# Windowed attention of a diffusion step: the loop over five query tiles written out as ten half tiles, with the next half's scores and exponentials issued ahead

## What is computed

```python
def _attend(q, k, v, valid, sink):
    s = jnp.einsum('bqgrd,bkgd->bgrqk', q, k).astype(jnp.float32) * (HEAD_DIM ** -0.5)
    if valid is not None:
        s = jnp.where(valid[None, None, None], s, NEG_INF)
    ...
    p = jax.nn.softmax(jnp.concatenate([s, sk], axis=-1), axis=-1)[..., :-1]
    return jnp.einsum('bgrqk,bkgd->bqgrd', p.astype(v.dtype), v)
```

## Time and profile before

| | |
|---|---|
| median of 3 runs | 5891.16 us (5883.75 to 5902.05) |
| the profiled execution's own time | 5885.15 us |
| its span | 5883.4 us |
| PE, PEld, DVE, ACT, POOL busy | 92%, 89%, 56%, 37%, 36% |
| attention of layer 0, first mask transfer to the end of the last copy | 385.32 to 504.83 us |
| attention of layer 1, the same | 3259.32 to 3379.23 us |

### The profile page before, as it was taken

How to read it: one execution, slowest core, us unless ns; L and a number is a source line. 1 busy time by engine, 2 the same in 40 slices (tenths; PEclk the granted TensorE clock), 3 DMA queues, 4 the chain that set the end, 5 groups by cost and what they waited for, 6 DMA issues and landing times. The chain is left out here.

```text
span 5883.4 us, 118582 instructions
## 1 busy us (share of the span) xinstructions
PE 5435.2 (92%) x47828; PEld 5219.4 (89%) x47828; DVE 3268.5 (56%) x6068; ACT 2201.4 (37%) x2769; POOL 2128.6 (36%) x968
## 2 busy tenths in 40 slices
PE   5977889899999999999989688889999999999999
PEld 2856779899999999999978477889999999999998
DVE  4545648665655156665645465586555631665665
ACT  4434322455555522222233433225555563222221
POOL 0001122466656443433400022136556654333332
PEclk8988999999999999999999799999999999999999
DMA  5200022355555564454411001124555546445443
GB/s 205 87 32 13 4 94 75 120 174 179 172 179 176 187 205 168 164 173 169 143 73 53 18 8 61 62 90 153 179 175 178 177 164 228 168 166 175 165 165 109
DMA packets 303987, 777.56 MB, mean 132 GB/s; under 512 B 23724, under 2 KB 109228, under 8 KB 299496
## 3 DMA queue, kind: packets, MB, share of 16 engines
q1 hardware_dynamic: 303592, 771.94, 38.7%
HBM read 586.52 MB, written 185.34 MB: 131 GB/s over the span
## 5 line engine op out<-in xcount | busy, mean ns | idle before, releaser
L2138 POOL TENSOR_TENSOR ex_v_lo<-ex_v_raw,ex_v_hi 128x1024 fp32r<-128x1024 f32 x256 | 691.6, 2723 | 1072.8 <-ACT ex_v_hi L2044 1072.8
L355 PE MATMUL ex_ps<-tk_h_hi,tk_u_hi 128*128 128x320 f32 x4096 | 965.7, 317 | 46.6 <-POOL tk_u_lo L2126 34.9
L2126 POOL TENSOR_TENSOR tk_u_lo<-tk_u_raw,tk_u_hi 128x1024 fp32r<-128x1024 f32 x256 | 642.2, 2509 | 883.3 <-ACT tk_u_hi L2014 862.0
L355 PE MATMUL ex_ps<-ex_wa_hi,ex_v_hi 128*128 128x320 f32 x4096 | 935.7, 310 | 18.8 <-issue 18.8
L355 PE MATMUL ex_ps<-tk_h_hi,tk_u_lo 128*128 128x320 f32 x4096 | 937.1, 310 | 0.0
L355 PE MATMUL ex_ps<-tk_h_lo,tk_u_hi 128*128 128x320 f32 x4096 | 935.8, 310 | 0.0
L355 PE MATMUL ex_ps<-ex_wa_lo,ex_v_hi 128*128 128x320 f32 x4096 | 935.1, 310 | 0.0
L355 PE MATMUL ex_ps<-ex_wa_hi,ex_v_lo 128*128 128x320 f32 x4096 | 934.9, 309 | 0.0
L2298 DVE TENSOR_TENSOR ex_y<-ex_y,ex_ps 128x640 f32<-128x640 f32 x496 | 405.9, 818 | 672.5 <-PE ex_ps L355 667.1
L355 PEld LDWEIGHTS ex_ps<-tk_h_hi,tk_u_hi 128*128 128x128 f32 x4096 | 679.0, 189 | 50.2 <-POOL tk_u_lo L2126 35.8
L355 PEld LDWEIGHTS ex_ps<-ex_wa_hi,ex_v_hi 128*128 128x128 f32 x4096 | 686.8, 188 | 19.3 <-issue 19.3
(11 more groups left out here) (326 smaller groups left out, 7836.7 us busy)
## 6 DMA issues: line engine op xcount, KB each, us to landing
tk_u_raw<-in_expert_u SPq DMA_DIRECT2D x256, 512.0 KB, 4.3
ex_v_raw<-in_expert_v SPq DMA_DIRECT2D x256, 512.0 KB, 3.3
act_spill<-tk_act_e SPq DMA_DIRECT2D x256, 320.0 KB, 2.3
grid_scratch<-tk_grid SPq DMA_DIRECT2D x160, 512.0 KB, 5.6
ex_g<-grid_scratch SPq DMA_DIRECT2D x64, 1280.0 KB, 10.6
x<-in_w_mod_rows SPq DMA_DIRECT2D x192, 256.0 KB, 5.1
ex_a<-act_spill SPq DMA_DIRECT2D x32, 1280.0 KB, 6.9
x<-act_spill SPq DMA_DIRECT2D x32, 1280.0 KB, 6.9
```

What stands on the lines that cost most here:

```text
L355: ins = nc.tensor.matmul(out[:, q, 0:HALF], a, b[:, q * HALF:(q + 1) * HALF], start=(first and n == 0), stop=(last and n == 2))
L2126: nc.gpsimd.tensor_tensor(u_lo[:, at % 2], u_raw[:, at % 3], u_hi[:, at % 2].bitcast(F32), ALU.subtract).then_inc(e["u_split"], 1)
L2138: nc.gpsimd.tensor_tensor(v_lo[h][:, k], v_raw[:, k], v_hi[h][:, k].bitcast(F32), ALU.subtract).then_inc(e["v_split"], 1)
```

## The change

The loop over tiles with its five stages becomes one stage without a loop. Its unit is the half tile: `part` 0 to 9, four heads each. The copies to `qs`, `ks`, `vs` are gone: with a constant index the matmuls read `z`, `k_tiles` and `v_tiles` directly. All five masks, 1280 KB, come in one transfer into the space of `rot`, which the stage before has finished with. `sm`, the buffer of scores and probabilities, has three slots of four heads, `ps_o` has two of one tile. Each engine's program does the next half's front work before the present half's back work. Nothing of the arithmetic is changed.

```diff
-        with nc.Fori(0, TILES) as m:
-            with stage(nc, "at_mask", "at_staged", "at_scores", "at_masked", "at_top", "at_exp",
...
+            @block.sync
+            def _(sp):
+                sp.dma_start(mask, s.d["masks"].rearrange("m p n -> p m n")).then_inc(mask_in, 16)
...
+                def score(part):
+                    m = part // 2
+                    for p in (2 * (part % 2), 2 * (part % 2) + 1):
+                        g = 8 * m + 2 * p
+                        if g >= 4:
+                            pe.wait_ge(masked, g - 2)
...
+                def turn(part, p):
+                    for n in (2 * p, 2 * p + 1):
+                        g = 4 * part + n % 4
+                        pe.wait_ge(probs, g + 1)
+                        if g >= 2:
+                            pe.wait_ge(pt_taken, g - 1)
...
+                def values(pair):
+                    m, p = pair // 4, pair % 4
+                    pe.wait_ge(pt_taken, 2 * pair + 2)
+                    if m >= 2:
+                        pe.wait_ge(out_taken, m - 1)
...
+                score(0)
+                for part in range(N):
+                    if part + 1 < N:
+                        score(part + 1)
+                    for q in range(2):
+                        turn(part, 2 * (part % 2) + q)
+                        if part or q:
+                            values(2 * part + q - 1)
+                values(2 * N - 1)
...
+                def front(part):
...
+                        dve.wait_ge(scores, 4 * part + h + 1)
+                        v.tensor_tensor_reduce(sm[:, part % SLOTS, h, :], ps_s[:, h, :], mask[:, part // 2, :], 1.0,
+                                               sink[:, h:h + 1], ALU.add, ALU.max, top[:, part, h:h + 1]).then_inc(masked, 1)
...
+                def back(part):
+                    dve.wait_ge(exped, 5 * part + 5)
...
+                def take(m):
+                    dve.wait_ge(out_ready, 8 * m + 8)
+                    v.tensor_copy(s.z[:, 0:4, m * P:(m + 1) * P], ps_o[:, m % 2]).then_inc(out_taken, 1)
...
+                front(0)
+                for part in range(N):
+                    if part + 1 < N:
+                        front(part + 1)
+                    back(part)
+                    if part and part % 2 == 0:
+                        take(part // 2 - 1)
+                take(TILES - 1)
...
+                exponents(0)
+                for part in range(N):
+                    if part + 1 < N:
+                        exponents(part + 1)
+                    copies(part)
```

More of the change, by code:

```diff
@@ L820, in attention @@
-        with nc.Fori(0, TILES) as m:
-            with stage(nc, "at_mask", "at_staged", "at_scores", "at_masked", "at_top", "at_exp",
[L822 to L834, removed]
+        ps_o = mem.enter_context(nc.psum_tensor("at_ps_o", [P, 2, 4, P], F32))
@@ L835, in values @@
                     for k in range(4):
                         for n in (2 * p, 2 * p + 1):
-                            v_k = (vs[:, k, :] if k < 3 else cv[:])[:, half(n)]
-                            ins = nc.tensor.matmul(ps_o[half(n), p, :], v_k, pt[:, n % 4, k * P:(k + 1) * P],
+                            v_k = (v_tiles[:, m + k, :] if k < 3 else cv[:])[:, half(n)]
+                            ins = nc.tensor.matmul(ps_o[half(n), m % 2, p, :], v_k, pt[:, n % 4, k * P:(k + 1) * P],
                                                    start=(k == 0), stop=(k == 3))
@@ L841, in values @@
                                 ins.then_inc(out_ready, 1)
[L843 to L881, removed]
-                        dve.wait_ge(masked, hs.stop)
-                        link(nc.vector.tensor_scalar(top[:, hs], top[:, hs], -1.0, None, ALU.mult))
-                        nc.vector.tensor_tensor(sink_e[:, hs], s.pvs("sink")[:, hs], top[:, hs],
-                                                ALU.add).then_inc(top_ready, 1)
-                    for n, hs in enumerate(head_halves):
-                        dve.wait_ge(exped, (n + 1) * (HEADS // 2 + 1))
-                        link(nc.vector.tensor_tensor(den[:, hs], den[:, hs], sink_e[:, hs], ALU.add))
-                        link(nc.vector.reciprocal(den[:, hs], den[:, hs]))
-                        for h in range(hs.start, hs.stop):
-                            nc.vector.tensor_scalar(sm[:, h, :], sm[:, h, :], den[:, h:h + 1], None,
-                                                    ALU.mult).then_inc(probs, 1)
-                    dve.wait_ge(out_ready, HEADS)
-                    nc.vector.tensor_copy(s.z[:, 0:4, bass.ds(m * P, P)], ps_o[:])
@@ new lines, in _, with exponents, copies @@
+            @block.scalar
+            def _(act):
+                def exponents(part):
+                    act.wait_ge(top_ready, part + 1)
+                    nc.scalar.activation(sink_e[:, part], sink_e[:, part], ACT.Exp).then_inc(exped, 1)
+                    for h in range(PART):
+                        nc.scalar.activation(sm[:, part % SLOTS, h, :], sm[:, part % SLOTS, h, :], ACT.Exp,
+                                             bias=top[:, part, h:h + 1], accum_out=den[:, part, h:h + 1]).then_inc(exped, 1)
+                def copies(part):
+                    for h in range(PART):
+                        g = 4 * part + h
+                        act.wait_ge(pt_ready, g + 1)
+                        if g >= 4:
+                            act.wait_ge(out_ready, g - 3)
+                        nc.scalar.activation(pt[:, h, :], ps_t[:, h % 2, :], ACT.Copy).then_inc(pt_taken, 1)
+                exponents(0)
[3 more added lines that the diff above has]
+                    copies(part)
```

67 lines of the change are left out of this document (44 added, 23 removed).

## The result

The changed kernel takes 5916.91 us, median of 7 runs (5908.67 to 5921.11), against 5891.79 for the kernel before on the same chip (7 runs). The ratio is 1.0032 with an interval of 1.0023 to 1.0041: **slower by 0.3%**, where I had said no change at 5882.5. (The two medians alone stand at 1.0043, a little above the interval of the recorded ratio; what follows needs only the direction.) The profiled execution took 5921.11 us with a span of 5919.3; before's span was 5883.4. The two profiles are 35.9 apart, the medians 25, since before's profiled execution was one of its short ones and the changed kernel's its longest.

What follows compares the result with a forecast made beforehand. No engine was full in attention; a chain passing between PE, DVE and ACT bounded it. Per layer 19.3 + 8 x 11.3 + 5.7 = 115.4 us, 8.6 less over both; forecast 5882.5 us, range 5858 to 5902.

Steps and rivals of the forecast that it cites:

- nothing else in the program moves: Whole kernel: barriers divide a layer's stages, so a microsecond saved in attention is one saved in the kernel.
- the long straight program loads late: Rival, attention: four additional rounds of code each cost a PE wait, at longest 6 us a layer; slower, chance 0.03.
- The half: Attention, one half tile: 10.1 us at full clock, 10.9 to 12.4 partly cold, mean 11.3, eight times a layer.
- two in nine: PE's clock in attention: after two of nine long pauses it stayed at 1.00; such halves cost 10.1 us.
- The order bound: Attention: DVE's `back` stands behind the next `front`, ACT's copies behind the next exponentials; turns wait some 3 us for DVE.
- the walk: Attention: step-by-step timing of one half through PE, DVE and ACT, from its first score; 10.1 us at full clock.
- The start: Attention's beginning: masks land at 5.2 us, first turn at 13.7, first half's values end at 19.3.
- the bounds: Attention's mask transfer: 1280 KB lands between 2.5 us, as 256 KB does, and 8.5, as 2560 KB does.
- The estimate of 7.7 us: Attention's mask transfer: 1280 KB by the skill's figure, making each layer 2.5 us longer; not used in the forecast.
- The clock did not hold: Rival, attention: PE's clock stays at 1.00 across pauses; halves 10.1 us, 104.9 a layer, 5861.6 in all; chance 0.35.
- The clock did not stay down: Rival, attention: PE cold throughout, 14.1 us a half, 142 a layer, 5936 us in all; chance 0.06.
- PE shows waits without a cause at regular distances: Sign in the changed trace that would show the prediction wrong; no size given.

Runs made afterwards that it cites:

- the loop put in place: Changed kernel with 96 more PE and 126 more DVE instructions, so the expert loops start elsewhere in a block: 0.9975, 5880.52 us.
- dummies: Changed kernel, expert loops moved by added code, with 16 unused identity turns in each of PE's nine attention pauses: 0.9953.
- the split transfer: Changed kernel, expert loops moved by added code, with the first tile's mask transferred by itself and the other four behind it: 0.9957.
- both together: Changed kernel, expert loops moved by added code; ACT copies before the next half's exponentials, DVE divides before masking the next half: 0.9920.
- ScalarE's by itself: Changed kernel, expert loops moved by added code; only ACT's order turned back, copies before the next half's exponentials: 0.9984.
- VectorE's by itself: Changed kernel, expert loops moved by added code; only DVE's order turned back, dividing before masking the next half: 1.0016.
- both additions: Kernel before with 40 PE instructions and 127 DVE memsets added ahead of the rotation of queries and keys: 1.0040.

## Why the prediction was wrong

**The step that failed** is a half sentence of the first part: "nothing else in the program moves". It was true of the diff and of the barriers between stages, and not of the place of the code. The stage's 1065 additional PE instructions moved the start of a later loop of 2940, whose first jump comes some 770 us behind attention. That cost 31.3 us over six jumps in the profiled executions, eleven times what attention gave. I had the jumps before me: before's list has 30.5 us for `issue` in the experts' matmuls, in 14 waits (two of them, 9.4 us each, outside the loop), and I looked only at those in the scan. The rival "the long straight program loads late" named the right resource at the wrong place, inside the stage, with at most 6 us a layer and a chance of 0.03. The sentence that I took from the Trainium skill (Runtime: NRT & Kernel Launch, Instruction fetch mechanics) for the straight code was not refuted: the list of waits has none of PE for `issue` within the ten halves. Its other half, that a taken branch can stall, is what the traces agree with (3.7 us at the loop's branch), and I used it for the branches that the change removes alone, not for those behind it.

**Attention** came out within 3% of the forecast time, 118.3 us in both layers against 115.4, but that left 2.8 us of the gain of 8.6 over 119.5 and 119.9 before. Term by term:

- *The half.* Forecast 11.3 on the mean, between 10.9 and 12.4. Eight intervals from the first turn at 400.58 to that at 493.20 are 11.58 on the mean, from 10.89 to 12.45; in layer 1 11.61. This term was 0.3 us too small, eight times, which is most of the 2.9. At full clock it is 10.2 against 10.1. The clock was at 0.76 on the mean, within the 0.7 to 0.85 expected; no half of layer 0's eight kept it (0.68 to 0.84), where I had counted on two in nine.
- *The order bound.* Turns led by DVE's scaling, 29.1 us in 9 waits of 3.3 at most against "some 3 us each"; DVE's maxima reach ACT late (49.0 us in 10). The loss to the two orders was named in the walk; the experiments show it, and show that neither gives anything without the other. ACT's copy held a turn back only once, for 1.7 us.
- *The start.* The masks landed after 6.1 us, not 5.2, and the first mask operation started 6.2 after the issue instead of 5.3. The first turn came at 14.2 instead of 13.7. The line between a small and a large transfer was 0.9 us too low; the bounds held.

```profile
PE at_ps_t L852 <- DVE at_sm L903: 29.1, 9, 3.3
...
PE at_ps_t L852 <- ACT at_pt L935: 1.7, 1, 1.7
```
```profile
DVE at_sm L889 <- DMA at_rot<-in_masks: 7.2, 1, 7.2
```

With these terms alone the time would have been 2.8 us below before, inside the range. With the loop put in place the changed kernel is at 0.9975, attention being 7.5 us shorter in that profile and the expert stage 5.4. The same attention thus gave some 3 us in one profile, with the clock at 0.76 in both layers, and 7.5 in another, with 0.78 and 0.82: a gain of this size depends on where the clock happens to fall. The estimate of 7.7 us, worked out from the Trainium skill's figure (DMA: Bandwidth & Descriptors, Measured), is 1.6 too many for this transfer, my 5.2 are 0.9 too few. That figure is of transfers issued from GpSimd; this one is issued by SP.

**The rivals.** The clock did not hold by itself; when made to hold, attention took 109.4 and 108.1 us, about 108 and 107 in the frame of the forecast, against the 104.9 of that rival: the start stays cold (0.85 in the first interval, 1.4 us longer than the others) and the masks are late. One layer without dummies, in the kernel with the split transfer, was at 0.93, so the rival was no idle one. The clock did not stay down either. The last sentence of the prediction had the sign of what came, "PE shows waits without a cause at regular distances", 200 us apart, but I had looked for them in attention.

## What to carry to other kernels

A change that adds or removes instructions moves every loop behind it. Where the list of waits shows `issue` at a loop's jump, work out how many instructions are added ahead of it, modulo a fetched block (256 here), and put a control with a few harmless instructions beside every comparison of some tenths of a per cent. And where two engines each hold back what the other needs, an order has to be tried on both together: here ScalarE's by itself gave nothing (0.9984 against 0.9975), VectorE's by itself was worse (1.0016), and both together gave 0.9920.

## What the runs showed of the hardware

The loop on PE of 2940 instructions pays at each jump: the branch takes 3.3 to 3.7 us (the medians of three kernels, 3.4 before), and PE resumes 1.6 to 1.9 us behind the landing of a 16,384-byte packet of instructions. A second wait ends 1.2 to 1.6 us behind the landing of the next. At the first jump of four kernels that is 4.9 to 5.5 us after PE resumed, and PE had 1.6, 1.7, 3.2 and 4.7 us of work until then; over all 42 such waits it is 3.5 to 6.3. The second loop on PE, of 789 instructions, has a branch of 0.2 us, and before's trace has no packet of the queue q8 between its first jump at 2200 us and 2999 us:

```profile
L2001 PEldq COMPARE_BRANCH  x30: 83/215/231, 2200.5 to 5866.2; - x30
```

Where between 789 and 2940 the cost begins, no run shows. Behind a second wait of 3.4 us the clock was at half for 4.5 us, and behind those of 2.3 and 2.0 us (20 and 16 instructions added) two matmuls came to take 0.73 us too; behind those of 1.8 us (both additions) and 0.5 us it stayed at full, 1.00 over the next 4 us. DVE's loop of 372 instructions was moved by 127 without effect. The wait of 17.6 us in six times that DVE shows for `issue` in the changed kernel stands in the one with the loop in place as well, which is faster than before in spite of it.
